# A two-layer streaming encoder on one core: two tiles of x and half of the keys' weights are made ready by the block in front of a layer

## What is computed

```
for l in range(DEPTH):                                    # DEPTH = 2
    h = rms_norm(x, g_norm[l])                            # x * rsqrt(mean(x*x) + eps) * g
    a_q, a_k, a_v, i_q, i_k, i_w, b_q, b_k, b_v, m_q, gate = split(h @ w_in[l])
    mk, mv = split(rms_norm(mem, g_mem[l]) @ w_mem_kv[l])
    o_a = attention over the 256 best keys of an indexer (8 heads, rotary)
    o_b = attention in a sliding window with sinks (4 heads, rotary)
    o_m = attention into 256 memory rows (4 heads)
    x = x + (concat(o_a, o_b, o_m) * silu(gate)) @ w_out[l]
y = rms_norm(x, g_final)
```

## Time and profile before

| | |
|---|---|
| time, median of 3 runs | 1576.17 us (1575.05 to 1578.86) |
| time of the profiled execution | 1578.83 us |
| its span in the trace | 1577.0 us |
| PE busy | 1393.8 us, 88% of the span |
| DVE busy | 933.0 us, 59% |
| ACT busy | 661.2 us, 42% |
| POOL busy | 154.3 us, 10% |
| moved by transfers | 108.60 MB, on average 69 GB/s |

### The profile page before, as it was taken

One profiled execution on the slowest core, in us unless ns is written; L12 is line 12 of the kernel. 1 busy time (PEld: TensorE's weight loads), 2 busy tenths in 40 slices (PEclk: granted clock), 3 DMA queues, 4 the chain that ended last, 5 costly groups with the idle time before them and its releaser, 6 DMA issues. The chain is left out here.

```text
span 1577.0 us, 19739 instructions
## 1 busy us (share of the span) xinstructions
PE 1393.8 (88%) x6364; PEld 780.9 (50%) x6364; DVE 933.0 (59%) x2699; ACT 661.2 (42%) x1667; POOL 154.3 (10%) x190
## 2 busy tenths in 40 slices
PE   5988789999959999998699887999997898999981
PEld 3444356566634445554444343566664454455450
DVE  1444636887655567876134436388875466777643
ACT  1123426776543334444011324377755243443342
POOL 1100013410000000000001000233000000000003
PEclk9998999999979999999789898999998799999996
DMA  6100420033041111111241014002133122111006
GB/s 202 53 25 18 138 69 2 2 133 95 29 120 54 61 54 55 54 48 34 58 169 53 11 32 163 27 1 107 42 95 107 35 72 84 53 56 54 28 11 250
DMA packets 89610, 108.60 MB, mean 69 GB/s; under 512 B 24016, under 2 KB 62640, under 8 KB 89520
## 3 DMA queue, kind: packets, MB, share of 16 engines
q1 hardware_dynamic: 89520, 107.45, 21.2%
HBM read 81.76 MB, written 25.76 MB: 68 GB/s over the span
## 5 line engine op out<-in xcount | busy, mean ns | idle before, releaser
L777 PE MATMUL score_ps<-w_slot,hT 128*128 128x512 f32 (+2 forms) x1024 | 394.8, 545 | 12.6 <-ACT prob_bm L1084 7.6
L777 PEld LDWEIGHTS score_ps<-w_slot,hT 128*128 128x128 f32 x1024 | 198.8, 197 | 195.3 <-issue 189.4
L777 PE MATMUL score_ps<-w_slot,work 128*128 128x512 f32 x512 | 230.8, 605 | 14.1 <-issue 14.1
L1278 DVE TENSOR_SCALAR_CACHE_REDUCE work<-bias,trial 128x384 f32<-128x384 f32 (+3 forms) x256 | 226.0, 883 | 6.9
L1000 ACT ACTIVATE work<-bias,neg_trial 128x768 bf16<-128x768 f32 (+2 forms) x192 | 198.4, 1043 | 67.4 <-DVE neg_trial L1274 67.4
L1150 ACT COPY work<-turn_ps 128x512 f32<-128x512 f32 (+1 forms) x102 | 57.7, 574 | 270.9 <-PE turn_ps L762 270.2
L777 PEld LDWEIGHTS score_ps<-w_slot,work 128*128 128x128 f32 x512 | 96.2, 193 | 135.4 <-issue 135.1
L848 PE MATMUL score_ps<-hT,w_slot 128*128 128x352 f32 x448 | 135.2, 460 | 1.4 <-ACT gate_raw L1114 1.4
L1130 ACT ACTIVATE hT<-hT,neg_top 128x128 f32<-128x128 f32 (+8 forms) x144 | 116.5, 811 | 16.6 <-DVE neg_top L1397 16.4
L1180 POOL TENSOR_TENSOR work<-work,norm_sb 128x512 f32<-128x512 f32 (+1 forms) x32 | 37.4, 1168 | 838.2 <-DMA norm_sb<-norm_scratch 838.2
L762 PE MATMUL turn_ps<-ident,hT 128*128 128x128 f32 (+1 forms) x720 | 95.5, 273 | 21.7 <-DVE hT L1458 15.2
(11 more groups left out here) (180 smaller groups left out, 1771.0 us busy)
## 6 DMA issues: line engine op xcount, KB each, us to landing
w_slot<-in_w_in_dram SPq DMA_DIRECT2D x8, 2048.0 KB, 10.1
gate_raw<-in_x_prompt_dram SPq DMA_DIRECT2D x16, 512.0 KB, 3.8
work<-gate_scratch SPq DMA_DIRECT2D x16, 512.0 KB, 4.8
x_scratch<-gate_raw SPq DMA_DIRECT2D x16, 512.0 KB, 3.6
gate_raw<-x_scratch SPq DMA_DIRECT2D x16, 512.0 KB, 3.7
norm_sb<-norm_scratch SPq DMA_DIRECT2D x56, 128.0 KB, 2.9
gate_scratch<-gate_raw SPq DMA_DIRECT2D x16, 264.0 KB, 3.1
gate_scratch<-gate_raw SPq DMA_DIRECT2D x8, 528.0 KB, 2.6
```

The source lines that it names most:

```text
L777: last = nc.tensor.matmul(out[:, 0:cols], lhs(k), w[:, k, 0:cols], start=(k == 0), stop=(k == KD - 1))
L1278: linked(nc.vector.tensor_scalar(tie_a[0:ROWS[t], 0:NKEYS[t]], scored(c), value[0:ROWS[t], c:c + 1], None, ALU.is_ge, ALU.add, accum_out=c ...
```

## The change

Tiles 0 and 1 of x no longer pass through `SQUARE` in a layer's list. They are loaded, summed, scaled and normalised ahead of the layer, in a buffer of their own (`head_x`, in `work`): for layer 0 by the opening block, for layer 1 by layer 0, in a new step `HEAD` that stands in front of the last two OUT steps. The first half of the keys' weights is loaded ahead too: for layer 0 by the opening block into `w_slot[0]`; for layer 1 by layer 0 into `head_w`, in the `bias` buffer, from where KEYS 0 to 3 read it, while `w_slot[0]` gets the same columns again for KEYS 4 to 8. The second half for layer 1 is issued by layer 0 behind its last store. `gamma` and the sinks are loaded by the block in front too (layer 0's sinks behind its other loads), and the rotary table moves from the opening block into layer 0. Tiles 2 and 3 are loaded without a wait in both layers.

The core of the diff (semaphores, and counts that shift by the two tiles, are left out):

```diff
-    return steps + [s for t, c in ((NT - 1, 1), (SMP, 0)) for s in (("OUT", t, c), ("ADD", t, c))]
+    return steps + [("HEAD", 0), ("HEAD", 1)] + [s for t, c in ((NT - 1, 1), (SMP, 0)) for s in (("OUT", t, c), ("ADD", t, c))]
...
-    steps = [("SQUARE", 0), ("SQUARE", 1), ("NORM", 0), ("NORM", 1)]
+    steps = [("NORM", 0), ("NORM", 1)]
...
+        head_x = [work[:, D_MODEL * n:D_MODEL * (n + 1)] for n in range(2)]
+        head_w = bias[:, 0:KD * 512].rearrange("p (k n) -> p k n", k=KD)
+        head_square = bias[:, KD * 512:KD * 512 + 512].bitcast(BF16)
...
+        def head_loads(sp, layer):
+            for n in range(2):
+                sp.dma_start(head_x[n], x_rows(n, layer)).then_inc(head_loaded[layer][n], 16)
+        def gamma_loads(sp, layer):
+            with nc.allow_non_contiguous_dma("per-feature scales, one per partition"):
+                for i, scales in enumerate((g_norm, g_mem)):
+                    sp.dma_start(gamma[:, i, :], scales[layer].rearrange("(k p) -> p k", p=P)
+                                 ).then_inc(head_params[layer], 16)
+        def sink_loads(sp, layer):
+            for h in range(B_HEADS):
+                sp.dma_start(sinks[layer][:, SLOT[h]:SLOT[h] + 1],
+                             sink[layer, h:h + 1].rearrange("(a n) -> a n", a=1).broadcast_to([P, 1])
+                             ).then_inc(sink_loaded[layer], 16)
+        def head_cols(sp, layer, i, dst):
+            c0, c1 = ((C_AK, C_IK), (C_IK, C_MQ))[i]
+            sp.dma_start(dst[:, :, 0:c1 - c0], w_in[layer, :, c0:c1].rearrange("(k p) n -> p k n", p=P)
+                         ).then_inc(head_w_loaded[layer][i], 16)
+        def head_squares(act, layer, n):
+            act.wait_ge(head_loaded[layer][n], 16)
+            if 2 * layer + n:
+                act.wait_ge(head_squared, 2 * layer + n)
+            nc.scalar.activation(head_square, head_x[n], ACT.Square, accum_out=sumsq[:, n:n + 1]
+                                 ).then_inc(head_squared, 1)
+        def head_rstds(pool, layer, n):
+            at = 2 * layer + n + 1
+            pool.wait_ge(head_squared, at)
+            nc.gpsimd.tensor_scalar(meansq[:, n:n + 1], sumsq[:, n:n + 1], 1.0 / D_MODEL, EPS, ALU.mult, ALU.add
+                                    ).then_inc(head_mean, 1)
+            pool.wait_ge(head_mean, at)
+            nc.gpsimd.tensor_tensor(rstd[:, n:n + 1], meansq[:, n:n + 1], half_neg[:, 0:1], ALU.pow
+                                    ).then_inc(head_rstd, 1)
+        def head_scales(dve, layer, n):
+            dve.wait_ge(head_rstd, 2 * layer + n + 1)
+            nc.vector.tensor_scalar(head_x[n], head_x[n], rstd[:, n:n + 1], None, ALU.mult).then_inc(head_normed, 1)
...
         with nc.Block() as block:
             @block.sync
             def _(sp):
-                sp.dma_start(rope_sb[:, 0:NT, :], rope_table[0:SEQ, :].rearrange("(t p) c -> p t c", p=P)
-                             ).then_inc(rope_loaded, 16)
-                sp.dma_start(rope_sb[0:DEC, SMP, :], rope_table[SEQ:NTOK, :]).then_inc(rope_loaded, 16)
-                sp.wait_ge(rope_loaded, 32)
+                head_loads(sp, 0)
+                gamma_loads(sp, 0)
+                head_cols(sp, 0, 0, w_slot[0])
+            @block.scalar
+            def _(act):
+                act.wait_ge(scales_made, 1)
+                for n in range(2):
+                    head_squares(act, 0, n)
+            @block.vector
+            def _(dve):
+                for n in range(2):
+                    head_scales(dve, 0, n)
 
             @block.gpsimd
             def _(pool):
+                nc.gpsimd.memset(sumsq[:, :], 1.0).then_inc(scales_made, 1)
+                nc.gpsimd.memset(half_neg[:, :], -0.5).then_inc(scales_made, 1)
...
+                pool.wait_ge(scales_made, 2)
+                for n in range(2):
+                    head_rstds(pool, 0, n)
...
-                        if n >= 2:
+                        if n >= 4:
...
-                    with nc.allow_non_contiguous_dma("per-feature scales, one per partition"):
-                        sp.dma_start(gamma[:, 0, :], g_norm[layer].rearrange("(k p) -> p k", p=P)
-                                     ).then_inc(params_loaded, 16)
-                        sp.dma_start(gamma[:, 1, :], g_mem[layer].rearrange("(k p) -> p k", p=P)
-                                     ).then_inc(params_loaded, 16)
-                    x_load(0)
-                    x_load(1)
-                    for h in range(B_HEADS):
-                        sp.dma_start(sink_sb[:, SLOT[h]:SLOT[h] + 1],
-                                     sink[layer, h:h + 1].rearrange("(a n) -> a n", a=1).broadcast_to([P, 1])
-                                     ).then_inc(params_loaded, 16)
-                    w_cols(0, C_AK, C_IK)
-                    w_cols(1, C_IK, C_MQ)
                     x_load(2)
                     x_load(3)
+                    if layer == 0:
+                        head_cols(sp, 0, 1, w_slot[1])
+                        sp.dma_start(rope_sb[:, 0:NT, :], rope_table[0:SEQ, :].rearrange("(t p) c -> p t c", p=P)
+                                     ).then_inc(rope_loaded, 16)
+                        sp.dma_start(rope_sb[0:DEC, SMP, :], rope_table[SEQ:NTOK, :]).then_inc(rope_loaded, 16)
+                        sink_loads(sp, 0)
+                    else:
+                        w_cols(0, C_AK, C_IK)
...
+                        if t == NT - 1 and layer + 1 < DEPTH:
+                            scores_taken(sp, ("QK", ITEMS.index((SMP, "A", 0)), 0))
+                            head_loads(sp, layer + 1)
+                            turn_taken(sp, ("NORM", NORMS - 1), 1)
+                            gamma_loads(sp, layer + 1)
+                            sink_loads(sp, layer + 1)
+                            head_cols(sp, layer + 1, 0, head_w)
                     x_store(SMP)
+                    if layer + 1 < DEPTH:
+                        head_cols(sp, layer + 1, 1, w_slot[1])
...
-                            pe.wait_ge(x_normed, n + 1)
+                            if n >= 2:
+                                pe.wait_ge(x_normed, n - 1)
+                            else:
+                                pe.wait_ge(head_normed, 2 * layer + n + 1)
+                            x = x_sb[n % 2] if n >= 2 else head_x[n]
                             for q in range(2):
-                                turn(step, q, [x_sb[n % 2][0:r, P * k:P * (k + 1)] for k in range(4 * q, 4 * q + 4)])
+                                turn(step, q, [x[0:r, P * k:P * (k + 1)] for k in range(4 * q, 4 * q + 4)])
...
-                            pe.wait_ge(w_loaded[0], 16 * (stage + 1))
+                            w0 = head_w if layer and kind == "KEYS" and t < 4 else w_slot[0]
+                            if stage or w0 is w_slot[0] and layer:
+                                pe.wait_ge(w_loaded[0], 16 * (stage + min(layer, 1)))
+                            else:
+                                pe.wait_ge(head_w_loaded[layer][0], 16)
+                            w1_loaded = (w_loaded[1], 16 * stage) if stage else (head_w_loaded[layer][1], 16)
...
-                            project(out[0:r, 0:512], 512, lhs, w_slot[0])
-                            pe.wait_ge(w_loaded[1], 16 * (stage + 1))
+                            project(out[0:r, 0:512], 512, lhs, w0)
+                            pe.wait_ge(*w1_loaded)
...
+                        elif kind == "HEAD" and layer + 1 < DEPTH:
+                            head_squares(act, layer + 1, step[1])
...
+                            if layer == 0 and t == 0:
+                                pool.wait_ge(rope_loaded, 32)
...
+                        elif kind == "HEAD" and layer + 1 < DEPTH:
+                            head_rstds(pool, layer + 1, step[1])
...
-                                dve.wait_ge(params_loaded, 16 * (2 + B_HEADS))
+                                dve.wait_ge(head_params[layer], 32)
...
+                            if layer == 0 and t == 0:
+                                dve.wait_ge(rope_loaded, 32)
...
+                        elif kind == "HEAD" and layer + 1 < DEPTH:
+                            head_scales(dve, layer + 1, step[1])
...
+                            if t == 0 and what == "B":
+                                dve.wait_ge(sink_loaded[layer], 16 * B_HEADS)
```

37 lines of the change are left out of this document (22 added, 15 removed).

## The result

The changed kernel took 1554.07 us (median of four runs, 1553.13 to 1555.10) against 1577.51 us of the kernel before in the same set: a ratio of 0.985 (95% interval 0.9835 to 0.9858), 23.4 us less. The forecast was 1557.8 us, 18.4 us less; the time lies in the range, at its lower part. The profiled execution took 1554.06 us, its span is 1552.3 us, 24.7 us shorter than before. Its transfers move 110.70 MB against 108.60, since layer 1's first half of the weights is loaded twice.

A forecast was written before the change was run, and what follows sets the result against it. Each layer's start was taken as a chain with one engine at work at a time; 5.9 (opening) + 11.5 (boundary) + 1.0 (clock) = 18.4 us off 1578.83 gives 1560.4, median 2.66 lower: 1557.8, range 1553 to 1564.

The forecast's parts named there:

- The opening's chain: Layer 0's start: tile 0 lands at 4.73, table load to 6.01, second tile normalised 10.33, first turn 10.70 us.
- Rival 4: Opening: the table load holds ACT longer than its row, its own 1.28 us again, giving 1559.1; chance 0.03.
- Turning two tiles: Both layers' starts: turning two tiles takes 4.78 us, so KEYS 0 starts at 15.5 and 782.4.
- The weights: Opening: first weights land about 13.5 us, second 20.6, wanted not before 23.3; late second weights costed at nothing.
- rival 2: Layer 0's weights come late, costing about 4.1 us, giving 1562; chance 0.21.
- The argument that the sinks would no longer stand ahead of them: Opening: four sink loads now stand behind the weights, one reason the 14.3 us landing was called pessimistic against about 13.5.
- The boundary: Layer 1's start: PE idle about 4.5 us instead of 12.8, KEYS 0 at 782.4 instead of 793.93, gain 11.5 us.
- rival 5: Layer 0's end waits for the head's loads, the sample's round trip is late, 1582 or more; chance 0.04.
- HEAD's work needs its cover: Layer 0's end: HEAD's 4.32 us chain on ACT, POOL and DVE is hidden; with the cover gone, 4.3 us.
- The clock: Both layers' starts: PE starts at 1.2 GHz; between nothing and 2.57 + 2.00 us can return, 1.0 us taken.
- rival 1: Layers' boundary: the clock stays up, some 3.3 us more gain, giving 1554.5; chance 0.13.

The follow-up runs named there:

- the early load in the opening: Changed kernel plus one ScalarE square before the wait for tile 0, so its function table loads early: 1553.48 us against 1555.55 for the changed kernel.
- boundary-alone kernel: Changed kernel with only the layers' boundary doing the new work, opening and layer 0's start as in the kernel before: 1565.23 us, ratio to before 0.9923.
- sinks-behind kernel: Kernel before with the four sink loads moved behind the caches in each layer: 1569.11 us against 1577.17, ratio 0.9948.
- The additions to the opening: Changed kernel with an early function table (1553.48 us) or, separately, 34 unused PE products in the opening (1554.99 us), against 1555.55.
- sinks-ahead kernel: Changed kernel with layer 0's four sink loads put back in front of the weights in the opening: 1562.55 us, ratio to before 0.9897.
- HEAD-last: Changed kernel with the step HEAD behind the last two OUT and ADD steps instead of in front: 1555.10 us against 1553.98.
- combined: Changed kernel plus early table, 34 unused opening products, second weights before tiles 2 and 3, 44 unused products ending layer 0: 1553.28 us against 1553.98.

## Why the prediction was right, and where its sizes were off

**The opening's chain** came within 0.12 us: first turn forecast at 10.70, measured 10.58; tile 0's landing 4.73 and 4.52, end of the chain 10.33 and 10.26. The function table stood on the path for its 1.28 us; taking it off moved the first turn by 1.3 to 1.6 us. Rival 4, that it holds ACT longer, is out: the squares began 0.01 us behind it, and the early load in the opening was over when its next instruction began at 2.02. The Trainium skill (ScalarE: Activation LUTs, What ACT_TABLE_LOAD costs) adds a drain of 1.38 us; the trace does not agree, here as at the gate.

**Turning two tiles was mis-sized**: 4.78 us in the sum, 3.77 measured, at both places, 1.0 us each. I took the stretch from the first turn to its end as PE's work. It held a wait of DVE for the sinks (1.42 us in the row of the boundary-alone kernel, 1.32 in before's own row of layer 1), which the sinks-behind kernel took away without any of the change (3.90 us). The row beside it, PE idle 1.60 us for DVE's hT, said that something was waited for, and I did not ask what DVE waited for.

**The weights** landed at 13.3 (forecast 13.5) and 21.2 (forecast 20.6); rival 2 did not come. But I had the second weights 2.7 us early (20.6 against 23.3), and they were some 0.1 us early (21.2 against 21.33), because turning and the clock were faster than forecast. The additions to the opening showed it: everything else that was made faster there ended in a wait for weights. The argument that the sinks would no longer stand ahead of them was worth more than I gave it: put back, they cost 3.5 us to KEYS 0 and 4.2 to 5.3 to KEYS 1.

**The boundary**: PE's pause forecast 4.5 us, measured 4.53; KEYS 0 9.3 us behind the last product, measured 8.30, the difference being the turning. The head's loads cost nothing: SP issued them from 717.89 to 724.9, the round trip started at 743.88 and PE's last two products follow each other; rival 5 is out. That HEAD's work needs its cover was too cautious for DVE's part, since the stores and the barrier behind the last product hide that as well.

**The clock was the second mis-sized term**: 1.0 us taken, 2.96 measured in the two KEYS 0 (2.03 and 0.93), and 2.2 more inside the layers. The forecast of its fall was right and rival 1's was not: it fell at the boundary in all four profiles. That the result, 1554.07, stands beside rival 1's 1554.5 is a coincidence of sizes. The 2.03 us in layer 0 go with PE's not standing still between turning and KEYS 0: there KEYS 0 took 13.10 to 14.23 us in the profiles without that pause whose weights did not break the row, and 14.84 to 16.04 behind pauses of 2.48 to 3.31 us. In the sinks-ahead kernel the granted clock shows it as well: PE stands still from 14.52 to 17.84, and the column reads 0.90 in 17 to 18 us, 0.50 from 18 to 21 and 1.00 again from 22 on. In before it reads 1.00 throughout that stretch, so there the cause is inferred from the durations. The 2.2 us inside the layers I cannot put down to the change: the one place that I could name is layer 0's first half of tile 7's output, 8.80 us in before and 7.10 in the changed kernel, and the boundary-alone, HEAD-last and combined kernels have 8.63 to 8.80 there, while the other ten profiles, the sinks-behind one among them, have 7.10 or 7.11. What decides it stays open.

Together: 17.4 us of starts were forecast and 19.5 came, 1.0 us of clock was forecast and 5.2 came. That the range held was in part luck: its lower end was rival 1's price and a margin, rival 1 did not come, and the two terms that were too small, turning and the rest of the clock, used up the room made for it.

## What to carry to other kernels

Before a head of work is moved into another block, look at what stands at the front of the transfer queue: a few loads of single elements can hold megabytes behind them, and here moving 2 KB in each layer to the back gave 8.1 us, over a third of the 22.9 that the whole change gave. When a stretch is carried over into a forecast as a duration, split it first into work and waits, by asking of each engine in it what its idle time was ended by. And when a start is pulled forward, work out what is late next with the optimistic durations, not the taken ones: here two faster pieces of the opening each ended in the same wait for the second half of the weights.
